# The first mixer's orders: scan pairs ahead of the next own products, memory rows and key splits on ScalarE, two parts of the output projection behind the last head

## The reference

```python
proj = xn @ w_in + b_in
q_h, v_h = to_heads(silu(h_q)), to_heads(h_i)              # HGRN: 4 heads of 128, both directions
hgrn_out = head_rmsnorm(o_h, hgrn_g, HGRN_HEADS) * silu(h_g)
qk = silu(centred_dwconv(concat([m_q, m_k]), conv_w, conv_b))    # 5 taps
h_m = mlstm_scan(...) + flip_seq(mlstm_scan(... flipped ...))
mlstm_out = head_rmsnorm(h_m, mlstm_g, MLSTM_HEADS) * sigmoid(m_o)
x = x + concat([hgrn_out, mlstm_out]) @ w_out
k, v = split(rmsnorm(mem, norm_mem) @ w_kv, 2)             # used by the cross attention
```

## Time and profile before

| | us |
|---|---|
| median of 3 runs (2099.19 to 2103.32) | 2102.91 |
| the profiled execution | 2102.18 |
| its span, first to last instruction | 2100.1 |
| TensorE busy in the span | 1986.9 |
| HGRN scan and the rest of the first mixer | 139 to 468 |

### The profile page before, as it was taken

One profiled execution on the slowest core, in us unless ns is written; L12 is line 12 of the kernel. 1 busy time (PEld: TensorE's weight loads), 2 busy tenths in 40 slices (PEclk: granted clock), 3 DMA queues, 4 the chain that ended last, 5 costly groups with the idle time before them and its releaser, 6 DMA issues.

```text
span 2100.1 us, 23451 instructions
## 1 busy us (share of the span) xinstructions
PE 1986.9 (95%) x9504; PEld 1433.5 (68%) x9504; DVE 808.3 (38%) x1211; ACT 539.5 (26%) x1119; POOL 1019.9 (49%) x580
## 2 busy tenths in 40 slices
PE   7998998989999999999999999999999999999987
PEld 6777886757877888888766767887864444434446
DVE  2545559462123410422564465554251222122235
ACT  4434436432222200211222342342120000000032
POOL 5786666726646877888553468445700000000015
PEclk9999998999999999999999999999999999999999
DMA  5321112312212333323321213212479999999971
GB/s 183 91 61 41 31 51 91 131 40 90 81 43 79 100 97 94 100 92 100 112 61 51 61 54 87 60 51 70 153 309 408 421 421 421 421 421 421 422 316 60
DMA packets 92410, 335.82 MB, mean 160 GB/s; under 512 B 7664, under 2 KB 9456, under 8 KB 67472
## 3 DMA queue, kind: packets, MB, share of 16 engines
q1 hardware_dynamic: 88432, 320.50, 41.7%
q10 hardware_dynamic: 3728, 13.30, 1.7%
q0 software_dynamic: 144, 0.52, 0.1%
HBM read 328.01 MB, written 6.29 MB: 159 GB/s over the span
## 4 chain that ended last, share of the span: by engine, by line
PE 75%; DVE 7%; DMA 7%; POOL 5%; ACT 3%; issue 2%; SPq 1%; PEldq 0%; ACTq 0%; DVEq 0%; PEld 0%; POOLq 0%
PE bank L558 48%; PE bank L1724 11%; DMA arena<-in_w_exp_up 4%; PE bank L1755 3%; PE bank L720 2%; DMA shared<-in_w_exp_down 1%; POOL shared_r L582 1%; DMA arena<-in_w_exp_gate 1%; POOL shared_r L583 1%; POOL shared_r L601 1%; PE bank L1392 1%; PE bank L1405 1%; PE bank L459 1%; PE bank L995 1%; DVE arena L1654 1%
## 5 line engine op out<-in xcount | busy, mean ns | idle before, releaser
L558 PE MATMUL bank<-shared_r 128*128 128x512 f32 (+1 forms) x4032 | 948.2, 391 | 21.2 <-POOL shared_r L583 10.4
L558 PEld LDWEIGHTS bank<-shared_r 128*128 128x128 f32 x4032 | 736.3, 192 | 192.0 <-issue 25.5
L582 POOL TENSOR_TENSOR shared_r<-shared,small 128x1024 fp32r<-128x1024 f32 (+1 forms) x184 | 358.4, 1948 | 944.5 <-DMA shared<-in_w_ple_gate 499.1
L583 POOL TENSOR_TENSOR shared_r<-shared,shared_r 128x1024 fp32r<-128x1024 f32 (+1 forms) x184 | 454.3, 2469 | 14.5
L1724 PE MATMUL bank<-arena 128*64 128x512 f32 x768 | 172.9, 595 | 12.6 <-DMA arena<-in_w_exp_up 5.2
L1724 PE MATMUL bank<-shared,arena 128*64 128x512 f32 x768 | 172.4, 599 | 5.9 <-DMA shared<-in_w_exp_down 2.5
L558 PE MATMUL bank<-shared_r,arena_r 128*128 128x512 f32 x768 | 176.1, 391 | 0.0
L650 DVE TENSOR_TENSOR X<-bank,X 128x512 f32<-128x512 f32 x96 | 61.1, 687 | 283.9 <-PE bank L558 186.8
L558 PEld LDWEIGHTS bank<-shared_r,arena_r 128*128 128x128 f32 x768 | 144.2, 188 | 31.5
L1724 PEld LDWEIGHTS bank<-arena 128*64 128x64 f32 x768 | 55.9, 137 | 122.5 <-issue 101.6
L1724 PEld LDWEIGHTS bank<-shared,arena 128*64 128x64 f32 x768 | 57.6, 138 | 112.6 <-issue 105.1
(11 more groups left out here) (390 smaller groups left out, 2099.2 us busy)
## 6 DMA issues: line engine op xcount, KB each, us to landing
shared<-in_w_in SPq DMA_DIRECT2D x80, 512.0 KB, 3.6
shared<-in_w_exp_gate SPq DMA_DIRECT2D x32, 1024.0 KB, 25.5
arena<-in_w_exp_gate SPq DMA_DIRECT2D x32, 1024.0 KB, 25.2
arena<-in_w_exp_up SPq DMA_DIRECT2D x32, 1024.0 KB, 24.9
shared<-in_w_exp_up SPq DMA_DIRECT2D x32, 1024.0 KB, 25.9
shared<-in_w_exp_down SPq DMA_DIRECT2D x32, 1024.0 KB, 26.2
arena<-in_w_exp_down SPq DMA_DIRECT2D x32, 1024.0 KB, 25.6
shared<-in_w_up SPq DMA_DIRECT2D x32, 512.0 KB, 3.7
```

Of the source, the lines that this page charges most:

```text
L558: ins = pe.matmul(dst, W_, x_, start=first, stop=final)
L582: link(pool.tensor_tensor(hi, raw(p), small[:, 18:19].to_broadcast([P, hi.shape[1]]), ALU.add))
L583: pool.tensor_tensor(lo, raw(p), hi.bitcast(F32), ALU.subtract).then_inc(S_("w_split"), 1)
```

## The change

- In the scan, VectorE's order at a chunk's end becomes query 5, pairs 3, query 6, pairs 4, own pairs.
- Memory rows: ScalarE squares them ahead of the last projection part's split and of the HGRN squares, and scales them itself (`Copy` with the scale, in place of VectorE's two instructions); VectorE does the root's input after two taps and the reciprocal after three. The four gate additions (L1159) are spread between the gate row's instructions, and the low halves of the memory come behind them.
- Keys: the product waits for the memory's evacuations part by part; from the third part on ScalarE makes the high halves and GpSimd the low ones. Both gate transposes go to one bank (4); the second key panel uses banks 5, 6, 7, 4.
- HGRN output: squares between the key splits, a root of their own, and scaling and gating in one set of 16 VectorE instructions.
- mLSTM: five value steps a head, the last at the start of the fourth; `turn_a` stands between the fourth head's scores and its cell outputs, its evacuations on VectorE are 0 and 1 ahead of the fourth head's outputs and 2 and 3 behind them; on ScalarE they and the sigmoids come behind the last exponentials. `turn_b` uses the right banks. In place of the dummies stand six steps of `out1`, and one more behind each of the first two transposes of `turn_b`.

The diff, cut (context and blank lines left out):

```diff
@@ -45,9 +45,9 @@
-          ("conv0", 4, LEFT), ("norm_mem", KT, LEFT), ("conv1", 4, LEFT), ("xk0", 4, RIGHT), ("gates", 2, RIGHT),
-          ("xk1", 4, RIGHT), ("xv", 4, RIGHT), ("spread", 2 * H, (0, 1)), ("mlstm", H * 2 * ST, (2, 3)),
-          ("turn_a", 4, RIGHT), ("turn_b", 4), ("out1", 8),
+          ("conv0", 4, LEFT), ("norm_mem", KT, LEFT), ("conv1", 4, LEFT), ("xk0", 4, RIGHT), ("gates", 1, (4,)),
+          ("xk1", 4, (5, 6, 7, 4)), ("xv", 4, RIGHT), ("spread", 2 * H, (0, 1)), ("mlstm", H * 2 * ST, (2, 3)),
+          ("turn_a", 4, RIGHT), ("turn_b", 4, RIGHT), ("out1", 8),
@@ -606,7 +606,7 @@
-    for name in ("proj_h", "proj_m"):
+    for name in ("proj_h", "proj_m", "xk"):
         for p in [p for w in range(PB[name], next_stage(name)) for p in panels[w]["parts"]][2:]:
@@ -927,9 +927,9 @@
-            own_pairs(m + 1)
...
+            own_pairs(m + 1)
         for j in range(ST):
@@ -954,15 +954,14 @@
-        bank_done(pe, BASE["norm_mem"] + KT - 1)
-        product(pe, PB["xk"], MEMTS, fm=True, toks=MEM)
+        product(pe, PB["xk"], MEMTS, fm=True, toks=MEM, ready=range(BASE["norm_mem"], BASE["norm_mem"] + KT))
         pe.wait_ge(S_("rows"), 1)
+        n = BASE["gates"]
+        bank = bank_claim(pe, n)
         for i, r in enumerate((RA, RE)):
-            n = BASE["gates"] + i
-            bank = bank_claim(pe, n)
             for j in range(ST):
-                ins = pe.transpose(bank[:, j * 64:(j + 1) * 64], r[0:64, j * P:(j + 1) * P], ident[0:64, 0:64])
-            bank_ready(ins, n)
+                ins = pe.transpose(bank[:, i * 256 + j * 64:i * 256 + (j + 1) * 64], r[0:64, j * P:(j + 1) * P], ident[0:64, 0:64])
+        bank_ready(ins, n)
@@ -977,14 +976,20 @@
+            if h == H - 1:
+                for _ in steps:
+                    pass
             pe.wait_ge(S_("conv"), 4 * (h // 2 + 1))
...
-                run_steps(steps, (0, 1, 0, 2)[s])
+                run_steps(steps, (0, 1, 0, 1)[s])
...
+            else:
+                pe.wait_ge(S_("mix_a"), 1)
+                mix_turn(pe, BASE["turn_a"], 0)
@@ -996,15 +1001,15 @@
-            if h == 2:
-                for _ in steps:
-                    pass
-                pe.wait_ge(S_("mix_a"), 1)
-                mix_turn(pe, BASE["turn_a"], 0)
-        keep_busy(pe, BASE["turn_b"], 6)
+        turned = [BASE["turn_a"] + d for d in range(4)] + [BASE["turn_b"] + d for d in range(4)]
+        steps = product_steps(pe, PB["out1"], XB, fm=False, ready=turned)
+        run_steps(steps, 6)
         for i in range(4):
...
+            run_steps(steps, i < 2)
+        for _ in steps:
+            pass
@@ -1029,16 +1034,17 @@
-    def conv_taps(dve, link, part):
-        for j in (0, 1, 3, 4):
+    def conv_taps(dve, link, part, taps):
+        for j in taps:
...
-        dve.sem_inc(S_("conv_y"), 4)
+        if taps[-1] == 4:
+            dve.sem_inc(S_("conv_y"), 4)
@@ -1056,41 +1062,53 @@
-        for c in range(ST):
-            for h in range(H):
-                act.activation(SQH[:, H * c + h, :], MIX[:, c, h * C:(h + 1) * C], ACT.Square, accum_out=head_ss[:, 2 * H * c + h:2 * H * c + h + 1])
-        split_hi(act, "proj_m", hi, 16)
         act.wait_ge(S_("mem_in"), 16)
...
+        split_hi(act, "proj_m", hi, 16)
         act.wait_ge(S_("ms_a"), 1)
-        act.activation(sd[:, 0:MT_], ms[:, 0:MT_], ACT.Sqrt)
-        act.activation(heads_of(head_ss, 0), heads_of(head_ss, 0), ACT.Sqrt).then_inc(S_("sd_a"), 1)
+        act.activation(sd[:, 0:MT_], ms[:, 0:MT_], ACT.Sqrt).then_inc(S_("sd_a"), 1)
+        act.wait_ge(S_("r_a"), 1)
+        for j in range(MT_):
+            ins = act.activation(MEMX[:, j, :], MEMX[:, j, :], ACT.Copy, scale=rstd[:, j:j + 1])
+        ins.then_inc(S_("mem_xs"), 1)
...
+        hi = [2]
+        split_hi(act, "xk", hi, 3)
...
-        keys_evacuate(act, 0)
+        split_hi(act, "xk", hi, 4)
         act.wait_ge(S_("mt"), 1)
...
-        for i, (dst, n) in enumerate(((ATM, BASE["gates"]), (ETM, BASE["gates"] + 1))):
-            bank = bank_take(act, n)
-            bank_release(act.activation(dst[:, :, :], bank[:, 0:256].rearrange("p (j r) -> p j r", j=ST), ACT.Copy), n)
+        split_hi(act, "xk", hi, 5)
+        def scan_squares(c):
+            for h in range(H):
+                ins = act.activation(SQH[:, H * c + h, :], MIX[:, c, h * C:(h + 1) * C], ACT.Square, accum_out=head_ss[:, 2 * H * c + h:2 * H * c + h + 1])
+            return ins
+        scan_squares(0)
+        keys_evacuate(act, 0)
+        split_hi(act, "xk", hi, 6)
+        n = BASE["gates"]
+        bank = bank_take(act, n)
+        for i, dst in enumerate((ATM, ETM)):
+            ins = act.activation(dst[:, :, :], bank[:, 256 * i:256 * i + 256].rearrange("p (j r) -> p j r", j=ST), ACT.Copy)
+        bank_release(ins, n)
...
-        act.wait_ge(S_("r_a"), 1)
-        for c in range(ST):
-            for h in range(H):
-                o = MIX[:, c, h * C:(h + 1) * C]
-                ins = act.activation(o, o, ACT.Copy, scale=head_r[:, 2 * H * c + h:2 * H * c + h + 1])
-        ins.then_inc(S_("mix_r"), 1)
-        for j in range(ST):
-            bank_done(act, BASE["proj_m"] + 12 + j)
-            ins = act.activation(GATE[:, j, 512:1024], GATE[:, j, 512:1024], ACT.Sigmoid)
-        ins.then_inc(S_("gate_b"), 1)
+        scan_squares(1)
+        split_hi(act, "xk", hi, 7)
+        scan_squares(2)
+        scan_squares(3).then_inc(S_("sq_h"), 1)
+        act.wait_ge(S_("ms_h"), 1)
+        act.activation(heads_of(head_ss, 0), heads_of(head_ss, 0), ACT.Sqrt).then_inc(S_("sd_h"), 1)
+        split_hi(act, "xk", hi, 8)
@@ -1112,10 +1130,16 @@
-                    head_squares(act, h - 1)
-                    if h == 3:
-                        for d in range(4):
-                            evac_hi(act, BASE["turn_a"] + d, XTS[:, 0, d, :], mix_gain(d))
+                    if h < 3:
+                        head_squares(act, h - 1)
+        head_squares(act, 2)
+        for d in range(4):
+            evac_hi(act, BASE["turn_a"] + d, XTS[:, 0, d, :], mix_gain(d))
+        for j in range(ST):
+            bank_done(act, BASE["proj_m"] + 12 + j)
+            ins = act.activation(GATE[:, j, 512:1024], GATE[:, j, 512:1024], ACT.Sigmoid)
+        ins.then_inc(S_("gate_b"), 1)
+        act.activation(small[:, 19:20], eps_, ACT.Sqrt)
@@ -1136,45 +1160,57 @@
-        split_parts_of(pool, link, "xk")
+        split_parts_of(pool, link, "xk", count=2)
+        split_lo(pool, link, "xk", [2], 8)
...
-        conv_taps(dve, link, 0)
+        conv_taps(dve, link, 0, (0, 1))
         dve.wait_ge(S_("sq_a"), 1)
-        dve.tensor_scalar(ms[:, 0:MT_], ss[:, 0:MT_], 1.0 / D, EPS, ALU.mult, ALU.add)
-        dve.tensor_scalar(heads_of(head_ss, 0), heads_of(head_ss, 0), 1.0 / P, EPS, ALU.mult, ALU.add).then_inc(S_("ms_a"), 1)
+        dve.tensor_scalar(ms[:, 0:MT_], ss[:, 0:MT_], 1.0 / D, EPS, ALU.mult, ALU.add).then_inc(S_("ms_a"), 1)
+        conv_taps(dve, link, 0, (3,))
         dve.wait_ge(S_("sd_a"), 1)
-        dve.reciprocal(rstd[:, 0:MT_], sd[:, 0:MT_])
-        link(dve.reciprocal(heads_of(head_r, 0), heads_of(head_ss, 0)))
-        dve.sem_inc(S_("r_a"), 1)
-        for j in range(MT_):
-            last = dve.tensor_scalar(MEMX[:, j, :], MEMX[:, j, :], rstd[:, j:j + 1], None, ALU.mult)
-        last.then_inc(S_("mem_xs"), 1)
-        for j in range(ST):
+        dve.reciprocal(rstd[:, 0:MT_], sd[:, 0:MT_]).then_inc(S_("r_a"), 1)
+        conv_taps(dve, link, 0, (4,))
+        def gate_b(j):
...
-        for d in range(KT):
-            evac_lo(dve, BASE["norm_mem"] + d, MEMTS[1][:, d, :], MEMTS[0][:, d, :], par("norm_mem", d), MEM)
+        def both(fn):
+            fn(slice(0, 4), slice(None))
+            return fn(slice(32, 36), slice(None, None, -1))
+        gate_b(0)
         dve.wait_ge(S_("ln_m"), 1)
...
-        def both(fn):
-            fn(slice(0, 4), slice(None))
-            return fn(slice(32, 36), slice(None, None, -1))
+        gate_b(1)
...
+        gate_b(2)
+        gate_b(3)
+        for d in range(KT):
+            evac_lo(dve, BASE["norm_mem"] + d, MEMTS[1][:, d, :], MEMTS[0][:, d, :], par("norm_mem", d), MEM)
...
-        conv_taps(dve, link, 1)
-        dve.wait_ge(S_("mix_r"), 1)
-        dve.tensor_tensor(MIX[:, :, 0:512], MIX[:, :, 0:512], GATE[:, :, 0:512], ALU.mult).then_inc(S_("mix_a"), 1)
+        conv_taps(dve, link, 1, (0, 1, 3, 4))
+        dve.wait_ge(S_("sq_h"), 1)
+        dve.tensor_scalar(heads_of(head_ss, 0), heads_of(head_ss, 0), 1.0 / P, EPS, ALU.mult, ALU.add).then_inc(S_("ms_h"), 1)
+        dve.wait_ge(S_("sd_h"), 1)
+        link(dve.reciprocal(heads_of(head_r, 0), heads_of(head_ss, 0)))
+        for c in range(ST):
+            for h in range(H):
+                o = MIX[:, c, h * C:(h + 1) * C]
+                r = 2 * H * c + h
+                ins = dve.scalar_tensor_tensor(o, o, head_r[:, r:r + 1], GATE[:, c, h * C:(h + 1) * C], ALU.mult, ALU.mult)
```

(13 more changed lines are left out.)

## The result

The changed kernel takes 2074.57 us (median of 4 runs, 2072.44 to 2079.06), the kernel before beside it 2101.05 (4 runs, 2094.4 to 2103.32). The ratio is 0.9882, with an interval of 0.9853 to 0.9911: faster by 1.2%, or 24.8 us, where 34 was forecast. 2069 was 5.6 us too low; the time lies within the range.

The account below looks back on a forecast made before the run. TensorE, busy 95% of the span, bounds the kernel; time comes only from its idle or low-clock stretches before 468 us. Scan 9, middle 11, value steps 1, last head 13 sum to 34: 2102.2 - 34 + 0.7 = 2069, range 2058 to 2085.

Parts of the forecast that it names:

- Scan, 9: HGRN scan, 139 to 316 us: pairs ahead of the own products save 9 us over seven chunk boundaries; bounds 4 and 14.
- Second, fourth, sixth and seventh: Scan's chunk boundaries: gains of 1.7, 1.4 and 1.7 where GpSimd itself waits for level 6, and 1.7 at the last.
- the third: Scan's chunk boundary near 204 us: 2.03 of wait and 1.5 of half clock behind it go, 3.5 us gained.
- the fifth: Scan's chunk boundary near 246 us: TensorE gains 1.5, then waits some 4; less a colder clock, 1.0 us gained.
- the first: Scan's chunk boundary near 157 us: GpSimd sets the pace, gain 0; a gap near 3 us risks the clock, loss of 2.
- Middle, 11: Scan's end to first mLSTM spread product, 316 to 383.71 us: memory rows and key splits faster, 11 us; bounds 4 and 14.
- Rival (a): Clock takes back the middle: key bursts all cold at 4.6 us, not 3.14; 2080 us; chance 0.19 together with ScalarE late.
- Rival (b): ScalarE late in the middle: key splits behind late gate rows, parts 4 to 7 3.5 later; 2078; 0.19 with the clock rival.
- The set of 16, nothing or at most 2: VectorE's merged scaling and gating ahead of the first mLSTM head: 4.29 us, covered by its wait; costs nothing, up to 2 uncovered.
- Last head and projection, 13: Third head's cells to the first projection product: 28.1 us becomes 14.4 with eight projection steps done; 13 kept, bounds 9 and 16.
- value steps, 1: mLSTM heads: one value step less per head, two behind the third head's last cells cover a 1.17 wait; 1.0 us.
- Rival (d): Projection's two parts delay something beside them, the last head gains only the dummies' 5 us; 2077 us; chance 0.07.

Follow-up runs that it names:

- e5_both: The changed kernel with scan output scaled on ScalarE, gated by one VectorE instruction in the second head, and memory evacuations ahead of the gate scans: 2059.43 us, ratio 0.981.

## Why the prediction was right, and where it failed

**The reading that the end is set by TensorE's idle time before 468 us, and that a shift is kept:** right, within the 3.6 us by which the part behind differs between executions. The norm transposes come 25.8 earlier, the last norm's dummies 29.5.

**Scan, 9:** measured 9.1, boundary by boundary as in the table. Second, fourth, sixth and seventh came within 0.3 of their figures, and the foreseen waits of some 3 and 4 us are there as 2.27 and 3.83. Three sizes were off: the third gave 2.4 and not 3.5; the fifth lost 0.8 where a gain of 1.0 was booked (behind its wait of 3.83 six matmuls took 2.93 and not 1.65); and the first kept its clock at 1.00 behind its gap and so gave 0.5 where a loss of 2 was booked. That they cancel to 0.1 is luck.

**Middle, 11:** measured 9.4. The step that failed is "That takes back half: the last evacuation comes at about 342.7, as before": it came at 346.0, 3.3 later. The prediction gives no price for the scans moved ahead of it; in its trace the pair took 2.44, and here 5.53 beside GpSimd. The key product itself did better than worked out, from 344.6 to 374.3 on the old axis, 29.7 us for 30.7. Rival (a), the clock taking the middle back, is out: it was 0.78 from 343 to 379 us before, and is 1.00 from 343 to 367 after. The rule of the Trainium skill weighed there (TensorE: Matmul & The Clock Gate, on HAM oscillation) did not decide here: the case that it describes has bursts shorter than the waits between them, and here bursts of 3.1 us at most 1.7 apart ran at the full clock. Rival (b), ScalarE late, is out too: the gate rows were done at 350.1 on the old axis, 5.4 earlier than before, and no key product waited more than 1.7 for its split.

**The set of 16, nothing or at most 2:** this is the step that cost the prediction its middle. "The two scalings of the scan's output merge into VectorE's 16 instructions (4.29 for a like set) ... Nothing. If that cover goes, it costs up to 2." The price was taken from a place where GpSimd was idle and used in one where GpSimd splits weights without a pause; it was 17.8, and 9.7 us of it came to stand on TensorE's path. The bound of 2 stands there without a working, and none was set for the price itself. At 4.29 the set, begun at 357.07, would have ended 1.9 before the spread product came; so the cover was there, and the price alone was wrong. The trace of before had warned: VectorE's L1154, two instructions of 128x1024, took 5.54 in the same stage beside GpSimd, and its scans of L1171 took 3.98 where those of L1169, of the same shape, took 2.44. L1154 reads only one tensor; a smaller one of its kind (L1172, 64x512) took 2.38 there and 0.42 in the changed kernel (L1200), where GpSimd was idle.

**Last head and projection, 13, and value steps, 1:** 15.2, and 14.1 alone. The stretch was costed at 14.4 with eight steps done at 25.4 after the first score; they were done at 23.7. The wait for ScalarE's evacuations, taken as 1.2 ahead of the third cell output, was 0.3. Rival (d), the projection's steps held up, is out: the first six took 8.3 for 8.2.

**The sum:** 9.1 + 9.4 + 15.2 is 33.7 for 34; less the 9.7 of one step booked at nothing, 24.0, beside 24.8 by the ratio. The mechanisms of the three parts held, and the two misses that cost most, the 9.7 and the 3.3 of the evacuations, have one cause: a price of VectorE's taken where GpSimd was idle. The time lies within the range, but the range was made of shortfalls elsewhere (5, 7 and 4), none of which came in that size; that it covers the 9.7 is luck. With the gating moved out and the evacuations put back in front, the same parts give 39.9 by the ratio (e5_both).

## What to carry to other kernels

When work moves between engines, take its price from a row with the same neighbours, not only of the same shape: for a VectorE instruction whose tensors all lie in SBUF, look at what GpSimd does in the place it goes to. Many small ones beside a GpSimd that never pauses are the worst form seen here, since about every second one waited out a GpSimd instruction; put them where GpSimd is idle. One large instruction among the same splits did well, but it began in a gap of GpSimd's, and what it costs behind a running one was not measured. And work that "only waits anyway" is free only until its successor is due: here the successor's bank was due 9.6 us before it came.
